# Condition: half the channels first, and three projection blocks begun inside the condition stage

## What is computed

```python
c_act = jax.nn.silu(c)
mod = c_act @ w_ada[l] + b_ada[l]                 # 6 x 1024 numbers
shift1, scale1, gate1, shift2, scale2, gate2 = split(mod, 6)
h = rmsnorm(x, g_norm1) * (1.0 + scale1) + shift1
... = split(h @ w_in, SPLIT_POINTS, axis=-1)      # 1024 x 8448 weights
```

## Time and profile before

| | us |
|---|---|
| median of three runs | 1897.28 (1896.14 to 1898.07) |
| the profiled execution, its own time | 1897.07 |
| its span in the trace | 1895.3 |
| TensorE busy | 1822.2 (96% of the span) |
| VectorE busy | 1516.1 (80%) |
| ScalarE, GpSimd busy | 729.4, 753.1 (38%, 40%) |

### The profile page before, as it was taken

One profiled execution on the slowest core, in us unless ns is written; L12 is line 12 of the kernel. 1 busy time (PEld: TensorE's weight loads), 2 busy tenths in 40 slices (PEclk: granted clock), 3 DMA queues, 4 the chain that ended last, 5 costly groups with the idle time before them and its releaser, 6 DMA issues. The chain is left out here.

```text
span 1895.3 us, 27336 instructions
## 1 busy us (share of the span) xinstructions
PE 1822.2 (96%) x9796; PEld 1600.4 (84%) x9796; DVE 1516.1 (80%) x2269; ACT 729.4 (38%) x979; POOL 753.1 (40%) x485
## 2 busy tenths in 40 slices
PE   4999989999899899998999999999899999999998
PEld 4888867777787888998999999999888888888886
DVE  7666467776447668989998989999768898888897
ACT  3322234444423321333333356666533333333233
POOL 0000088000032000567988878888323343334330
PEclk7999999999999999999999999999999999999999
DMA  8899368878495071559999979999999999999993
GB/s 314 267 326 330 129 189 234 241 222 265 155 282 151 4 156 22 164 173 272 304 294 310 289 265 341 342 360 347 339 383 390 390 390 391 392 393 390 390 390 121
DMA packets 306615, 526.24 MB, mean 278 GB/s; under 512 B 21690, under 2 KB 211691, under 8 KB 301932
## 3 DMA queue, kind: packets, MB, share of 16 engines
q1 hardware_dynamic: 269676, 391.11, 63.6%
q0 software_dynamic: 36864, 134.23, 20.2%
HBM read 438.75 MB, written 85.99 MB: 277 GB/s over the span
## 5 line engine op out<-in xcount | busy, mean ns | idle before, releaser
L125 PE MATMUL u_s<-h_hi,u_hi 128*128 128x384 f32 x1024 | 349.1, 341 | 9.6 <-POOL u_lo L1984 5.8
L126 PE MATMUL u_s<-h_lo,u_hi 128*128 128x384 f32 x1024 | 344.4, 336 | 0.0
L127 PE MATMUL u_s<-h_hi,u_lo 128*128 128x384 f32 x1024 | 343.9, 336 | 0.0
L125 PE MATMUL v_o<-v_v_hi,v_w_hi 128*128 128x512 f32 x768 | 300.1, 391 | 6.8 <-DVE v_w_lo L2278 5.8
L127 PE MATMUL v_o<-v_v_hi,v_w_lo 128*128 128x512 f32 x768 | 299.5, 390 | 0.0
L126 PE MATMUL v_o<-v_v_lo,v_w_hi 128*128 128x512 f32 x768 | 299.5, 390 | 0.0
L1984 POOL TENSOR_TENSOR u_lo<-u_ut,u_hi 128x1024 fp32r<-128x1024 f32 x79 | 197.2, 2496 | 55.8 <-ACT u_hi L1767 55.2
L125 PEld LDWEIGHTS u_s<-h_hi,u_hi 128*128 128x128 f32 x1024 | 193.3, 189 | 12.2 <-issue 7.0
L126 PEld LDWEIGHTS u_s<-h_lo,u_hi 128*128 128x128 f32 x1024 | 193.4, 189 | 0.0
L127 PEld LDWEIGHTS u_s<-h_hi,u_lo 128*128 128x128 f32 x1024 | 193.1, 189 | 0.0
L1415 POOL DMA_INDIRECT rows_buf<-in_u_experts_dram,few_idx x117 | 157.9, 1350 | 88.0 <-DMA v_gt<-expert_gates 63.4
(11 more groups left out here) (348 smaller groups left out, 4017.8 us busy)
## 6 DMA issues: line engine op xcount, KB each, us to landing
u_raw<-in_u_experts_dram SPq DMA_DIRECT2D x320, 128.0 KB, 4.9
v_raw<-in_v_experts_dram SPq DMA_DIRECT2D x74, 512.0 KB, 11.7
v_slot<-in_v_experts_dram SPq DMA_DIRECT2D x54, 512.0 KB, 12.2
expert_acts<-u_ao SPq DMA_DIRECT2D x64, 384.0 KB, 6.7
u_raw<-turned_experts SPq DMA_DIRECT2D x24, 1024.0 KB, 7.2
expert_gates<-u_gs SPq DMA_DIRECT2D x12, 2048.0 KB, 8.7
v_gt<-expert_gates SPq DMA_DIRECT2D x30, 768.0 KB, 17.1
w_in_raw<-in_w_in_dram SPq DMA_DIRECT2D x17, 1024.0 KB, 11.8
```

The source lines that it names most:

```text
L125: nc.tensor.matmul(out, w[0], x[0], start=first, stop=False)
L126: nc.tensor.matmul(out, w[0], x[1], start=False, stop=False)
L127: return nc.tensor.matmul(out, w[1], x[0], start=False, stop=last)
```

## The change

- Load order: `w_ada` block 0, block 2 (shift and scale of channels 0 to 511), three weight blocks, then `w_ada` blocks 1 and 3, then the small vectors of lambda; weight block 3 waits for the last sum.
- `w_ada` block 0 goes to TensorE alone (`direct`); blocks 2, 1 and 3 are summed on VectorE in full. Each half of the channels gets its coefficients as soon as its own sums are there (`modulated(0)`, `modulated(1)`).
- x is moved out of the accumulators as `xnt` for all 512 tokens; the modulation then goes by channel group (128 channels, 512 tokens) instead of by token block. ScalarE makes `h_hi` from `xnt` directly, VectorE makes the full value `hf` and `h_lo`.
- The low parts of the three first weight blocks are made by GpSimd, in six pieces of 128x1024; ScalarE makes their high parts in the same pieces.
- TensorE multiplies block 0, 1 and 2 over channel groups 0 to 3, then block 0 over groups 4 to 7. In the projection `rest(1)` and `rest(2)` add groups 4 to 7; `product(3)` is the first block of the old form, with its `split_lo(3)` at its old place in VectorE's list.
- Two of the four squares of x and one of the four scalings go to, or stay on, ScalarE, the others run on VectorE.

```diff
-OWN_ROWS = 2
+FIRST = 3
+def half_product(pe, nc, acc, w, keep, low_ok, cs, done=None):
+    for c in cs:
+        pe.wait_ge(low_ok, c + 1)
+        for m in range(2):
+            ms = slice(m * P, (m + 1) * P)
+            ins = three(nc, acc[m], (w[0][:, c, ms], w[1][:, c, ms]), (keep["h_hi"][:, c, :], keep["h_lo"][:, c, :]), c == 0, c == KD - 1)
```

SyncE in the condition stage:

```diff
+            ada_block(0)
+            ada_block(2)
+            for b in range(FIRST):
+                weights(b)
+            ada_block(1)
+            ada_block(3)
...
+            sp.wait_ge(mod_mm, 2)
+            weights(FIRST)
...
+        parts = [(b, h) for h in range(2) for b in range(FIRST)]
```

GpSimd:

```diff
+            for n, (b, h) in enumerate(parts):
+                pool.wait_ge(w_hi_ok, n + 1)
+                ks = half_of(h)
+                nc.gpsimd.tensor_tensor(first[b][1][:, ks, :], raw[b][:, ks, :], first[b][0][:, ks, :].bitcast(F32), ALU.subtract).then_inc(w_lo_ok, 1)
```

ScalarE:

```diff
+            split_hi(0)
+            split_hi(1)
...
+            high(0)
+            for n in range(2, len(parts)):
+                split_hi(n)
+            high(1)
```

VectorE:

```diff
+            def full(c):
+                nc.vector.tensor_scalar(hf[:, c % 4, :], xnt[:, c, :], keep["scale1"][:, c:c + 1], keep["mod"][:, c:c + 1], ALU.mult, ALU.add).then_inc(hv_ok, 1)
+            def low(c):
+                dve.wait_ge(hi_ok, c + 1)
+                dve.wait_ge(hv_ok, c + 1)
+                nc.vector.tensor_tensor(keep["h_lo"][:, c, :], hf[:, c % 4, :], keep["h_hi"][:, c, :].bitcast(F32), ALU.subtract).then_inc(low_ok, 1)
...
+            accumulate(0, 2)
...
+            modulated(0)
+            accumulate(1, 1)
+            accumulate(2, 3)
+            modulated(1)
```

TensorE in the condition stage:

```diff
+            half_product(pe, nc, acc_of[0], first[0], keep, low_ok, range(0, 4))
...
+            half_product(pe, nc, acc_of[1], first[1], keep, low_ok, range(0, 4))
+            shares(1, CB)
...
+            half_product(pe, nc, acc_of[2], first[2], keep, low_ok, range(0, 2))
+            shares(2, KD + CB).then_inc(mod_mm, 1)
+            half_product(pe, nc, acc_of[2], first[2], keep, low_ok, range(2, 4))
...
+            half_product(pe, nc, acc_of[0], first[0], keep, low_ok, range(4, KD), mm)
```

VectorE in the projection stage, inside `turn`:

```diff
-                split_lo(4 * i + 1, 1)
-                if not first:
+                    split_lo(4 * i + 1, 1)
                     dve.wait_ge(order_ok, i)
                 shares(i, range(0, 5))
                 turn_rows(4 * i)
-                split_lo(4 * i + 2, 2)
+                if not first:
+                    split_lo(4 * i + 2, 2)
```

TensorE in the projection stage:

```diff
-            first_product(nc, acc, parts, keep, 1, mm)
-            for b in range(1, 4):
-                product(b, b, b < 2)
+            for b in range(1, FIRST):
+                rest(b)
+            product(FIRST, FIRST)
```

More of the change, by code:

```diff
@@ L174, in weight_parts, with phase_condition @@
     return space[:, :, :].rearrange("p (x a) b -> p x (a b)", x=4).rearrange("p x (k n) -> p x k n", k=KD)
-OWN_ROWS = 2
[L180 to L184, removed]
+FIRST = 3
[3 more added lines that the diff above has]
+        for m in range(2):
             ms = slice(m * P, (m + 1) * P)
[L186 to L191, removed]
+            ins = three(nc, acc[m], (w[0][:, c, ms], w[1][:, c, ms]), (keep["h_hi"][:, c, :], keep["h_lo"][:, c, :]), c == 0, c == KD - 1)
+            if c == KD - 1:
+                ins.then_inc(done, 1)
+def phase_condition(nc, a, keep, raw, w_in, first, pairs, mm):
     with ExitStack() as stack:
@@ L302, in _ @@
             rstd_dve_out(nc, dve, dve_c, root[:, :], fin[:, :], fac_ok)
-            dve.wait_ge(sil_ok, 1)
[L304 to L312, removed]
@@ L319, in _ @@
[L319 to L326, removed]
@@ L328, in _ @@
[L328 to L332, removed]
+            dve.wait_ge(fac_ok, 1)
+            for i in range(3):
+                nc.vector.tensor_scalar(xn[:, i, :], x[:, i, :], root[:, i:i + 1], None, ALU.mult).then_inc(xn_dve, 1)
+            for i in range(2):
+                dve.wait_ge(x_t, i + 1)
+                nc.vector.tensor_copy(xnt[:, :, i * P:(i + 1) * P], p_x[i]).then_inc(xt_dve, 1)
@@ L354, in transposes, with direct @@
                 ins.then_inc(x_t, 1)
-            transposes(0)
-            transposes(1)
-            def shares(cs):
+            def direct(cs):
                 for c in cs:
-                    ins = nc.tensor.matmul(p_mod[:, c:c + 1], acc[:, c // KD, c % KD * P:(c % KD + 1) * P], keep["ones"][:, 0:1], start=True, stop=True)
-                return ins
+                    for x in range(KD):
+                        nc.tensor.matmul(p_mod[:, c:c + 1], ring[0][:, x, c * P:(c + 1) * P], keep["csil"][:, x:x + 1], start=x == 0, stop=x == KD - 1)
@@ L363, in _, with shares @@
+            def shares(n, at):
+                pe.wait_ge(acc_c.sem, KD * n + KD)
+                for c in range(CB):
+                    ins = nc.tensor.matmul(p_mod[:, at + c:at + c + 1], acc[:, n, c * P:(c + 1) * P], keep["ones"][:, 0:1], start=True, stop=True)
+                return ins
+            for i in range(2):
+                pe.wait_ge(xn_dve, i + 1)
+                transposes(i)
             pe.wait_ge(sil_ok, 1)
[L364 to L367, removed]
@@ L377, in _ @@
[L377 to L385 removed]
+            for h in range(2):
+                pe.wait_ge(ada_in[0][h], 16)
+            direct((0, 1))
+            pe.wait_ge(xn_dve, 3)
@@ new lines, in _ @@
+            pe.wait_ge(xt_dve, 1)
+            transposes(2)
+            pe.wait_ge(xn_act, 1)
+            pe.wait_ge(xt_dve, 2)
+            transposes(3)
+            direct((2, 3))
+            shares(0, KD).then_inc(mod_mm, 1)
+            acc_of = [[pairs[b][:, m * S:(m + 1) * S] for m in range(2)] for b in range(FIRST)]
+            pe.wait_ge(w_lo_ok, 1)
+            half_product(pe, nc, acc_of[0], first[0], keep, low_ok, range(0, 4))
+            pe.wait_ge(w_lo_ok, 2)
+            pe.wait_ge(xt_act, 2)
```

194 lines of the change are left out of this document (110 added, 84 removed).

## The result

The changed kernel takes 1905.29 us (median of 7, 1903.31 to 1911.12), the one before 1896.66 in the same comparison: ratio 1.0058, interval 1.0048 to 1.0068, so it is 8.6 us slower. The profiled execution took 1903.31, span 1901.5; the seven times fall into two groups, 1903.3 to 1905.3 (four executions) and 1910.2 to 1911.1 (three).

What follows compares the result with a forecast made beforehand. Loads and VectorE were taken to bound the condition stage, TensorE's matmuls the projection. Block 3's start at 89.0 plus 2.6 for the clock, less 80.7 before, gave +10.9: 1897.1 + 10.9 = 1908.0 us, range 1895.0 to 1912.0.

Steps and rivals of the forecast that it cites:

- half clock: TensorE at block 3 of the projection: restart at half speed after a 10.8 us pause, costing 2.6 us.
- the lock: Condition stage: GpSimd and VectorE take turns on two-input SBUF work, each waiting the other's whole instruction, 2.41 us per piece.
- To the first coefficients: Start of the condition stage: loads, squares, transposes, column matmuls and first sum; coefficients at 28.1 us instead of 26.8.
- Boundary: End of the condition stage, where the projection begins: at 67.3 us, before at 53.0.
- Block 3: Projection: first matmul of weight block 3 at 89.0 us, 21.7 after the boundary, after 10.8 us of TensorE idling.
- The reason given for block 3: Projection: its low part did not move in VectorE's list; two removed splits preceded a load ending later anyway, giving nothing.
- no lock: Rival: GpSimd and VectorE run side by side in the condition stage; boundary 54.3, time 1895.0 us; chance 0.17.
- 19 groups: No-lock rival: TensorE's count of channel groups in the condition stage, worked without waiting, ending at 53.8 us.
- The partial lock: Rival: VectorE held only two or three times, 6 us instead of 13; boundary near 60, time 1901.5; chance 0.15.
- The clock: Rival: TensorE's clock stays at half through the condition stage, adding 14.4 us, time 1922; chance 0.04.

Runs made afterwards that it cites:

- e10: The changed kernel with GpSimd's six subtractions replaced by one-input copies of the same size; 1899.20 us, one execution.
- e2: The changed kernel with its six low parts made by VectorE and nothing on GpSimd; 1902.56 us.
- e11: The changed kernel with GpSimd's six subtractions replaced by memsets of the same size, low parts left out; 1905.12 us, one execution.
- e12: The changed kernel itself, run again for another profile; 1906.36 us.
- e3: The changed kernel with block 3's split first, block 4's load first in the projection stage and its split after five steps of the sums; 1915.22 us.
- e1: The changed kernel with the split of block 3 as first step of VectorE's projection list; 1909.22 us.
- e5: The changed kernel with the projection's first two w_ada blocks and weight blocks 4, 5 and 6 loaded inside the condition stage; 1903.72 us.
- e6: The changed kernel with the early loads of e5 and the six low parts on VectorE; 1898.56 us, ratio to before 1.0010.
- e8: The changed kernel with e5, e2 and e7 together; 1895.39 us, ratio to before 0.9994.
- e9: e8 with block 3's split first and the load of block 6 back behind the boundary; 1892.93 us, ratio to before 0.9983.
- e7: The changed kernel with half of w_ada block 0's columns summed by VectorE, TensorE multiplying two columns instead of four; 1908.90 us.

## Why the prediction was right, point by point

The forecast was 1908.0 against 1905.29, in its range and on the right side. The kinds of cost were right: GpSimd holding VectorE, a late boundary, block 3 waiting for its split, half clock after it. That the size came so near is partly luck. Without the lock the boundary was forecast at 54.3, and e10, with copies in place of the subtractions, has 58.9; the lock was forecast to cost 13.0 there (67.3 against 54.3), and costs 6.0 to 7.2 between like starts. The two misses nearly cancel.

- **To the first coefficients:** forecast 28.1, measured 31.2. VectorE's sum was over at 24.6 as said. The mis-sized step is "its 32 matmuls of one column 4.05": the program's 32 appear as 64 in the trace, two groups of 3.83 and 3.93, and I charged TensorE with one. Its serial chain from 13.95 to 29.9 was the bound, and VectorE idled 5.4 us. The added table load cost what I kept, 1.28: the activation starts 1.29 after the load's start.
- **The lock:** right in kind, shown by e2, e10 and e11, wrong in place. I had "the five other GpSimd pieces" fall into `full` and `low`, 12 us. Because the coefficients were late, the second piece was over before them. The last four could hardly fall there: their high parts stand behind `high(0)` in ScalarE's list, and `high(0)` itself waits for the coefficients, which I left out. They hit the next sum and took 8.2 us, and 0.8 went on `scale1`. VectorE's turn per piece was as said: three steps of `L338` took 8.4 us from 38.10, one step for each GpSimd piece of 2.7.
- **Boundary:** 67.3 forecast, 65.5 measured, by the two misses above.
- **Block 3:** boundary + 21.7 forecast, + 22.8 measured; the load that it goes by was used 16.9 after the boundary (82.38 above), for 16.1 before. Idle 10.8 against 11.69; half clock 2.6 against 2.0. Together 10.9 forecast, 9.6 measured at the last ones-sum. The rest of the 2.7 lies in the later stages, which differ between executions: from the last ones-sum to the end it is 1669.4 us before, 1666.1 in the changed kernel's profile, 1668.6 in e12, and up to 1670.8 in the others, e3 (1674.6) apart.
- **The reason given for block 3** was incomplete. I named its place in VectorE's list and a load "that ends later anyway". e1 shows that the place is worth nothing while loads and sums of the first turn begin at the boundary. The kernel before waits nowhere in the stage: its 174.6 us are TensorE's own work. The change takes 16.5 us of that work out (158.1 are left: 171.8 less 11.69 and 2.0), and 13.7 come back as waiting and half clock. So the boundary moves 12.4 later and the stage shortens by only 2.8. Only the runs that start the loads earlier (e5, e6, e8, e9) shortened it further, by 6 to 7; of the 6.6 to 7.7 still left above 158.1, e5 shows the wait for expert rows.
- **Rivals:** no lock fell with the profile and e2. Its "19 groups" should read 16, four each for three blocks and four more of block 0; its 53.8 goes with 16. The partial lock came nearest to the size (6 us, for 6.0 to 7.2 at the boundary) and was still wrong on how: every piece beside a busy VectorE was paid. The clock was back within 4.5 us each time.

## What to carry to other kernels

Work that is moved ahead of a barrier moves the barrier: ask which loads are first issued behind it, and how long the DMA engines stand still in front of it. When a wait is taken away at one consumer, look at the next instruction of the same engine (here the ones-sum) before the gain is counted. Before work of a second engine is placed beside a busy one, follow what feeds it through its own queue: here ScalarE's list, not the loads, set when GpSimd's last four pieces ran. A GpSimd instruction that reads SBUF is free only while VectorE idles, and an edit that fills VectorE's idle time can turn it into a cost, as e7 did.

## What the runs showed beyond that

The clock column does not always show what the matmuls show. In e2 the column stands at 1.00 over the whole stretch from 10 to 46 us, while one-column matmuls take 0.21 and products of 512 columns start every 0.43, as at half clock; at 42.3 they change to one every 0.23. A stretch and a piece of TensorE's timeline of e2:

```profile
10.00:46.00 36.00, 30.25 (x131) 28.39 (x132) 24.14 (x41) 15.84 (x20) 0.00 (x0) 1.00 0.89 310
```

```profile
41.06 0.63 PE L125 MATMUL proj_acc<-h_hi,proj_hi 128*128 128x512 f32 x1
41.48 0.63 PE L126 MATMUL proj_acc<-h_lo,proj_hi 128*128 128x512 f32 x1
41.91 0.59 PE L127 MATMUL proj_acc<-h_hi,proj_lo 128*128 128x512 f32 x1
42.33 0.39 PE L125 MATMUL proj_acc<-h_hi,proj_hi 128*128 128x512 f32 x1
42.56 0.39 PE L126 MATMUL proj_acc<-h_lo,proj_hi 128*128 128x512 f32 x1
```

So in these profiles the spacing of matmuls is the surer sign; I take the 1.00 for a missing record, which no run proves. Transposes hardly show the clock: those of two token blocks take 3.52 in the changed kernel where the column stands at 1.00 (10 to 17 us), 3.40 where it stands at 0.50 (21 to 24 us), and 3.65 in e2.
